# Transfer pieces at other places, the gated output's first product ahead of the stage boundary, tile differences and left remainders moved from GpSimd to VectorE

## The reference

```python
x = x + mixer(rmsnorm(x, norm_mix[i])) @ w_out[i]
h = rmsnorm(x, norm_ffn[i])
g = causal_dwconv(h @ w_gate, conv_w, conv_b)          # D_FF = 2816
x = x + (gelu(g) * (h @ w_up)) @ w_down
gate = sigmoid(rmsnorm(x, norm_ple[i]) @ w_ple_gate[i])
x = x + gate * (p[i] @ w_ple_proj[i])                  # p: 1024 x 256
```

## Time and profile before

| | |
|---|---|
| median of 3 runs | 3132.71 us (3130.48 to 3138.84) |
| the profiled execution | 3134.82 us, span of the core 3133.0 us |
| TensorE busy in the span | 3009.1 us (96%), weight loads 2506.6 us (80%) |
| VectorE, ScalarE, GpSimd busy | 2253.6 (72%), 1440.7 (46%), 1392.6 us (44%) |
| mean granted clock of TensorE | 0.988 of full speed |
| right-sum transfers, GpSimd's queue | 24 pieces, 1408 KB, median 10.2 us to landing |
| gate weights of the up pass | 11 loads a layer, 1024 KB, median 7.4 us to landing |

### The profile page before, as it was taken

How to read it: one execution, slowest core, us unless ns; L and a number is a source line. 1 busy time by engine, 2 the same in 40 slices (tenths; PEclk the granted TensorE clock), 3 DMA queues, 4 the chain that set the end, 5 groups by cost and what they waited for, 6 DMA issues and landing times. The chain is left out here.

```text
span 3133.0 us, 44207 instructions
## 1 busy us (share of the span) xinstructions
PE 3009.1 (96%) x14830; PEld 2506.6 (80%) x14830; DVE 2253.6 (72%) x3461; ACT 1440.7 (46%) x3127; POOL 1392.6 (44%) x913
## 2 busy tenths in 40 slices
PE   7999999999999989999999999999999999999999
PEld 6778888988877778878788887899877777877877
DVE  5599997888377778789943331999557677789962
ACT  4384537878243333344432211888443333344441
POOL 3105545564245555524322544676235555543330
PEclk9999999999999999999999999999999999999999
DMA  5313334222324552475311334323123564266511
GB/s 179 124 56 105 95 122 102 47 65 64 135 77 154 136 128 84 133 264 183 97 55 41 105 98 142 76 65 74 54 82 126 155 129 114 92 210 221 160 59 50
DMA packets 288086, 349.07 MB, mean 111 GB/s; under 512 B 88316, under 2 KB 181292, under 8 KB 287916
## 3 DMA queue, kind: packets, MB, share of 16 engines
q1 hardware_dynamic: 274860, 312.27, 31.7%
q0 software_dynamic: 13056, 34.60, 5.2%
HBM read 268.70 MB, written 112.20 MB: 122 GB/s over the span
## 5 line engine op out<-in xcount | busy, mean ns | idle before, releaser
L2171 DVE TENSOR_SCALAR_CACHE_REDUCE k_x<-k_x,l0in_cand,l0in_want 128x384 bf16<-128x384 f32 (+1 forms) x186 | 174.9, 1003 | 1.2 <-DVE l0in_before L2166 0.2
L2661 POOL TENSOR_TENSOR l0ff_w_lo<-l0ff_raw_g,l0ff_w_hi 128x512 fp32r<-128x512 f32 x64 | 90.3, 1414 | 163.2 <-ACT l0ff_w_hi L2519 162.1
L2661 POOL TENSOR_TENSOR l1ff_w_lo<-l1ff_raw_g,l1ff_w_hi 128x512 fp32r<-128x512 f32 x64 | 90.3, 1414 | 161.4 <-ACT l1ff_w_hi L2519 160.3
L78 PE MATMUL l1in_acc<-k_w_lo,k_hi 128*128 128x512 f32 x384 | 150.9, 393 | 2.4 <-PEq L99 2.4
L79 PE MATMUL l1in_acc<-k_w_hi,k_lo 128*128 128x512 f32 x384 | 150.1, 391 | 0.0
L80 PE MATMUL l1in_acc<-k_w_hi,k_hi 128*128 128x512 f32 x384 | 150.0, 391 | 0.0
L2548 ACT ACTIVATE k_x<-k_x 128x512 f32<-128x512 f32 x88 | 55.6, 631 | 170.9 <-DVE k_x L2753 170.9
L2709 DVE TENSOR_TENSOR l0ff_w_lo<-l0ff_raw_u,l0ff_w_hi 128x512 fp32r<-128x512 f32 x65 | 62.2, 957 | 83.0 <-ACT l0ff_w_hi L2519 83.0
L2709 DVE TENSOR_TENSOR l1ff_w_lo<-l1ff_raw_u,l1ff_w_hi 128x512 fp32r<-128x512 f32 x65 | 62.2, 957 | 79.7 <-ACT l1ff_w_hi L2519 79.7
L721 DVE TENSOR_TENSOR l1in_sq<-l1in_out 128x512 f32<-128x512 f32 x32 | 38.4, 1202 | 107.9 <-ACT l1in_out L658 107.5
L1632 DVE TENSOR_TENSOR l1dil_pt_lo<-l1dil_ring,l1dil_pt_hi 128x512 fp32r<-128x512 f32 x192 | 101.9, 553 | 4.7 <-ACT l1dil_pt_hi L1568 2.3
(11 more groups left out here) (663 smaller groups left out, 11291.6 us busy)
## 6 DMA issues: line engine op xcount, KB each, us to landing
l_right_sums<-in_w_down POOLq DMA_DIRECT2D x24, 1408.0 KB, 10.2
acts<-k_x SPq DMA_DIRECT2D x88, 256.0 KB, 2.0
k_raw<-in_w_in_odd SPq DMA_DIRECT2D x24, 512.0 KB, 3.9
l0ff_raw_g<-in_w_gate SPq DMA_DIRECT2D x11, 1024.0 KB, 7.4
l0ff_raw_u<-in_w_up SPq DMA_DIRECT2D x11, 1024.0 KB, 8.7
l0ff_a<-acts SPq DMA_DIRECT2D x44, 256.0 KB, 5.4
l0ff_d_one<-in_w_down SPq DMA_DIRECT2D x44, 256.0 KB, 3.0
l1ff_raw_g<-in_w_gate SPq DMA_DIRECT2D x11, 1024.0 KB, 7.4
```

The costliest lines, as they stand in the source:

```text
L78: pe.matmul(out, a_hi, b_lo, start=start, stop=False)
L2171: tick(dve.tensor_scalar(hits[:, cols], score[:, cols], cand[:, i:i + 1].bitcast(F32), want[:, i:i + 1], ALU.is_ge, ALU.add, accum_out=exc ...
L2661: pool.tensor_tensor(buf.ring_lo[q % R][:], operand(q), buf.ring_hi[q % R][:].bitcast(F32), ALU.subtract).then_inc(w_lo_done[0], 1)
```

## The change

1. The twelve right-sum pieces of a layer are issued at n = 2 and 12 of groups 1 to 6 (copies 1 to 3, adds 4 to 6).
2. The first gate product of `ple_stage` (24 matmuls) is done by TensorE at the end of `ffn_stage`, once tiles 0 and 1 and the gate weights' first half are ready. A pair of banks, `gate_bank`, lives across three stages for that: in the output stage it takes the transposes of odd tiles, in the feed-forward stage it is the second half of the up banks, in the last one it is `ps_g`. Unit 0 of `ple_stage` leaves its gate product out.
3. In the output stage GpSimd makes the differences of tile 4 alone. VectorE's first `sums_of` in the feed-forward stage covers tiles 5 and 6 in instructions of twice the width.
4. From down step 6 on VectorE makes every left remainder, GpSimd none.

```diff
@@ output_stage
-        tp = st.ps("tp", [P, 4, 512])
-        banks = [[tp[:, 2 * i + h, :] for h in range(2)] for i in range(2)]
+        tp = st.ps("tp", [P, 2, 512])
+        banks = [[z[:, h, :] for h in range(2)] for z in (tp, spare)]
...
-            for t in range(NT // 2, NT // 2 + 2):
-                nfeed.differences(pool, t)
+            nfeed.differences(pool, NT // 2)
@@ ple_stage
-        ps_g = st.ps("ps_g", [P, 2, 512])
+        ps_g = buf.bank
...
                 act.wait_ge(filled, i + 1)
                 if i == 0:
+                    act.wait_ge(begun, 1)
...
-                for k in range(KD):
+                for k in range(KD if i else 0):
@@ ffn_stage
-        LOWS.append([n + (z >= 6 and z % 2 == who if who else not (z >= 6 and z % 2)) for who, n in enumerate(LOWS[-1])])
+        LOWS.append([n + ((z >= 6) == bool(who)) for who, n in enumerate(LOWS[-1])])
...
-        bank = [buf.bank, st.ps("bank_u", [P, 4, 512])]
-        ups = bank[1]
+        bank_u = st.ps("bank_u", [P, 2, 512])
+        ups = [z[:, i, :] for z in (bank_u, nxt.bank) for i in range(2)]
+        bank = [[buf.bank[:, i, :] for i in range(4)], ups]
...
-                if n in (6, 13) and grp < 6:
-                    i = 2 * (grp % 3) + (n == 13)
-                    right_sums.copy(pool, i) if grp < 3 else right_sums.add(pool, i)
+                if n in (2, 12) and 1 <= grp <= 6:
+                    i = 2 * ((grp - 1) % 3) + (n == 12)
+                    right_sums.copy(pool, i) if grp <= 3 else right_sums.add(pool, i)
...
-            def sums_of(t):
-
-                at = slice((t - NT // 2) * P, (t - NT // 2 + 1) * P)
+            def sums_of(t, end):
+
+                at = slice((t - NT // 2) * P, (end - NT // 2) * P)
...
-            sums_of(LAST - 1)
+            sums_of(LAST - 2, LAST)
...
             for z in range(Z):
                 down(z)
+            pe.wait_ge(n_lo_ready, KD // 2)
+            pe.wait_ge(nfeed.rested, 4)
+            for k in range(KD):
+                mm = mm3(pe, nxt.bank[:, 0, :], nxt.hi[:, nxt.slot(0), k, :], nxt.lo[:, nxt.slot(0), k, :], nxt.x_hi[0][:, k, :], nxt.x_lo[0][:, k, :],
+                         k == 0, k == KD - 1)
+            mm.then_inc(begun, 1)
```

More of the change, by code:

```diff
@@ L845, with __init__ @@
     ROOTS = 4
-    def __init__(self, st, hi, lo, gain, w_gate, w_proj, p_in):
-        self.p_in = p_in
+    def __init__(self, st, bank, hi, lo, gain, w_gate, w_proj, p_in):
+        self.bank, self.p_in = bank, p_in
         self.gain, self.w_gate, self.w_proj, self.hi, self.lo = gain, w_gate, w_proj, hi, lo
@@ L2350, in ffn_stage @@
         a22 = cells("a22", (34, 38, 66, 70, 8, 10, 12, 14, 20, 22, 24))
-        bank = [buf.bank, st.ps("bank_u", [P, 4, 512])]
-        ups = bank[1]
+        bank_u = st.ps("bank_u", [P, 2, 512])
+        ups = [z[:, i, :] for z in (bank_u, nxt.bank) for i in range(2)]
+        bank = [[buf.bank[:, i, :] for i in range(4)], ups]
         NF = len(buf.FACTORS)
-        out = lambda grp, f, m: bank[m][:, (NF * grp + buf.FACTORS.index(f) + 2 * m) % 4, :]
-        feed = SplitFeed(st, x, hi, lo, xt, [None, [ups[:, 0, :], ups[:, 1, :]]], ident, buf.gain, buf.norm, buf.AHEAD, buf.ROOTS, "f_")
-        nfeed = Feed(st, x, nxt.hi, nxt.lo, [[ups[:, 2 * i + h, :] for h in range(2)] for i in range(2)], ident, nxt.gain, nxt.norm,
+        out = lambda grp, f, m: bank[m][(NF * grp + buf.FACTORS.index(f) + 2 * m) % 4]
+        feed = SplitFeed(st, x, hi, lo, xt, [None, ups[0:2]], ident, buf.gain, buf.norm, buf.AHEAD, buf.ROOTS, "f_")
+        nfeed = Feed(st, x, nxt.hi, nxt.lo, [ups[0:2], ups[2:4]], ident, nxt.gain, nxt.norm,
                      slot=nxt.slot, tag="n_")
@@ L2814, in add @@
                     dve.wait_ge(added, ADDED[r])
-                dve.tensor_tensor(cols, cols, bank[r % 2][:, n % 4, :], how).then_inc(added, 1)
+                dve.tensor_tensor(cols, cols, bank[r % 2][n % 4], how).then_inc(added, 1)
             def low_left(z):
@@ L2967, in _ @@
             pe.wait_ge(feed.rounded, 2)
[L2968 removed]
+            pe.transpose(ups[1][:, 0:4 * NFB], cw4, ident[0:4 * NFB, 0:4 * NFB]).then_inc(cw_t, 1)
             for q in range(4, Q):
@@ L3047, in trunk @@
                 recycle(nc)
-            with Stage(nc, L + "ff") as fs, Stage(nc, L + "pg") as gs:
-                ple = PleBuffers(gs, chain_hi, chain_lo, a["norm_ple"][layer], a["w_ple_gate"][layer], a["w_ple_proj"][layer], a["p"][layer, 0])
-                buf = FfnBuffers(fs, a["norm_ffn"][layer], a["w_gate"][layer], a["w_up"][layer], kept)
-                kept_stored = [nc.alloc_semaphore(f"{L}_kept_stored{b}") for b in range(2)]
-                filled = nc.alloc_semaphore(f"{L}_filled")
-                output_stage(nc, L + "out", merged, out_buf, ident, x, buf, kept_stored, filled, a["x"][0] if even else None)
-                recycle(nc)
-                Stage.used.extend(kept_stored + [filled])
-                ffn_stage(nc, L + "ff", x, buf, ple, right_sums[layer], a["conv_w"][layer], a["conv_b"][layer], ident, acts, kept_stored, filled)
@@ L3057, in trunk @@
-            recycle(nc)
-            if even:
-                ple_stage(nc, L + "pg", x, ple, ident, nxt=heads)
-                recycle(nc)
-            else:
-                ple_stage(nc, L + "pg", x, ple, ident, final=out[0])
+            with Stage(nc, L + "gate") as bs:
+                gate_bank = bs.ps("bank", [P, 2, 512])
+                with Stage(nc, L + "ff") as fs, Stage(nc, L + "pg") as gs:
+                    ple = PleBuffers(gs, gate_bank, chain_hi, chain_lo, a["norm_ple"][layer], a["w_ple_gate"][layer], a["w_ple_proj"][layer], a["p"][layer, 0])
+                    buf = FfnBuffers(fs, a["norm_ffn"][layer], a["w_gate"][layer], a["w_up"][layer], kept)
+                    kept_stored = [nc.alloc_semaphore(f"{L}_kept_stored{b}") for b in range(2)]
+                    filled = nc.alloc_semaphore(f"{L}_filled")
+                    begun = nc.alloc_semaphore(f"{L}_begun")
+                    output_stage(nc, L + "out", merged, out_buf, ident, x, buf, gate_bank, kept_stored, filled, a["x"][0] if even else None)
+                    recycle(nc)
+                    Stage.used.extend(kept_stored + [filled])
+                    ffn_stage(nc, L + "ff", x, buf, ple, right_sums[layer], a["conv_w"][layer], a["conv_b"][layer], ident, acts, kept_stored, filled, begun)
+                recycle(nc)
+                Stage.used.append(begun)
+                if even:
+                    ple_stage(nc, L + "pg", x, ple, ident, begun, nxt=heads)
+                    recycle(nc)
+                else:
+                    ple_stage(nc, L + "pg", x, ple, ident, begun, final=out[0])
```

15 lines of the change are left out of this document (7 added, 8 removed).

## The result

| | before | after |
|---|---|---|
| median | 3131.9 us | 3092.6 us (3090.6 to 3096.6) |
| the profiled execution, span | 3134.8, 3133.0 us | 3093.5, 3091.7 us |
| VectorE, GpSimd busy | 2253.6, 1392.6 us | 2238.8, 1269.5 us |
| mean granted clock | 0.988 | 0.993 |

The ratio is 0.9872, with a 95% interval of 0.9854 to 0.989: 1.3% faster, 40 us. The forecast was 3078.4 us, 14 us too low, inside its range; the nearest case of the prediction is rival (a), 3092.

The account below looks back on a forecast made before the run. TensorE works nearly all the time, so only its waits and slow clock can be won. 3134.8 - 50.7 + 8.2 - 3.6 - 8.2 = 3080.5 us, 3078.4 on the median's scale; range 3062 to 3102.

Parts of the forecast that it names:

- rival (a): Up pass: the add's tail still holds up its gate load, gaining 37 us for 50.7, so 3092 us; chance 0.15.
- Part 1: Up pass: moved right-sum pieces let gate loads land in time, gaining 50.7 of 52.6 us lost in both layers.
- within the 9.8: Up pass: a gate load landing up to 9.8 us after issue does no harm to the next group's first product.
- bound of 52.6: Up pass: the most the moved pieces could gain, all the time lost in both layers, 52.6 us.
- The other bound, 37: Up pass: the least gain, 37 us, if three loads per layer each meet their add for half its length.
- Part 2: Gated output: the early product moves the boundary later and unit 2 waits for VectorE's multiplication; +8.2 us in both layers.
- The half clock: Gated output: TensorE's 4.7 us stand ahead of unit 2 brings the half clock, 2.4 us more in layer 0.
- Part 3: Output stage's end: VectorE ends sooner, the next stage begins 1.5 us earlier; -1.8 us per layer, -3.6 in all.
- a tile's chain that sets the pace: Head of the feed-forward stage: scale, transpose, round and remainder set the pace, leaving a gain of 1.8 us per layer.
- Part 4: Down pass: VectorE making all left remainders at 2.65 us a step speeds steps and shrinks a TensorE wait; -8.2 us.
- Rival (d): Down pass: VectorE stands every step until ScalarE has rounded the left operand; +85 us, so 3172 us; chance 0.05.

Follow-up runs that it names:

- adds_at_0: The changed kernel with one add per group at n = 0 of groups 4 to 9, copies left as they are: 3073.9 us, ratio 0.9801.
- sigmoid_first: The changed kernel with ScalarE's roundings of weight chunks 2 to 4 put behind the sigmoids of units 0 to 2: 3087.1 us, ratio 0.9845.

## Why the prediction came out as it did

**Part 1**: forecast -50.7, measured -42.3 alone and -38.1 in the changed kernel (U). The direction and most of the size were right: the six gate loads that meet an add land after 6.6 to 8.4 us, where 7.7 to 8.3 was said (the slowest two of layer 0 in the changed kernel, 1072.5 to 1075.5 and 1114 to 1118, of each the gate load):

```profile
l0ff_raw_g<-in_w_gate SPq DMA_DIRECT2D x1, 1024.0 KB, 7.7
```
```profile
l0ff_raw_g<-in_w_gate SPq DMA_DIRECT2D x1, 1024.0 KB, 8.4
```

That this figure came out is in part luck. The undisturbed landing of 6.7 us was the slowest of eight loads in the kernel before with no piece in flight; the other seven took 5.3 to 5.6. The overlap with the add was 1.8 to 4.1 us, not 2 to 3, and it cost some 0.7 us per us in the changed kernel, not 0.5. The too high base and the too low price offset each other.

What failed is the step from "within the 9.8" to "gained". The slack was read for one consumer, product 0 of the next group, in a group that nothing had disturbed. Product 0 was on time; product 5, whose remainder VectorE makes, was not. I also asked only what the add does to the gate loads, and not to the stores, though the add of place 12 is in flight just when they go out. GpSimd's issue was priced at nothing, and with it at place 12 VectorE's next multiplication takes 3.9 to 4.4 us in place of 1.2. And I closed the account at group 7: the lag reaches the down pass, where the kernel before lost 2.6 and 1.1 us as well, so that U could shrink by 56.3 us (adds_at_0), more than my bound of 52.6. The other bound, 37 for loads that meet half an add, came close for a reason that isn't the one given.

**Part 2**: forecast +8.2 against a gain that the edit is meant to bring. Measured about +8.9 by the stretches. The chain was named rightly: it starts at the boundary, not at the product, and unit 2 starts 17.2 us behind the boundary in layer 0 (17.3 was said for the multiplication's end), after a wait of 2.75 us, and of 4.41 in layer 1, where 4.7 was said. The half clock was counted behind this wait in layer 0 too; in this execution it came there in layer 1 alone, where unit 2's product, 5.5 us at full clock, took 8.07 (window, busy us by engine, then the clock, the share of transfer engines and GB/s):

```profile
2984.00:2992.07 8.07, 8.07 (x25) 6.40 (x25) 5.96 (x6) 1.63 (x3) 2.37 (x1) 0.67 0.42 130
1559.93:1565.51 5.58, 5.58 (x24) 4.61 (x25) 5.54 (x6) 1.64 (x3) 2.40 (x1) 1.00 0.64 188
```

The next stage began 5.9 us after the early product did (5.76 was said), the wait at the boundary was 0.33 us where the earlier trace rows had 2.85, and sigmoid_first shows the cause of the other one: ScalarE's queue.

**Part 3**: forecast -3.6, measured -2.9. VectorE's last operations before the boundary are at 0.68 us, where 1.74 stood in the earlier trace rows:

```profile
884.43 0.68 DVE L808 TENSOR_TENSOR l0ff_xt<-l0ff_xt 128x512 f32<-128x512 f32 x1
885.03 0.68 DVE L804 TENSOR_TENSOR l0ff_lo<-l0ff_xt,l0ff_hi 128x512 fp32r<-128x512 f32 x1
885.63 0.68 DVE L998 TENSOR_TENSOR l0ff_lo<-l0ff_xt,l0ff_hi 128x512 fp32r<-128x512 f32 x1
```

The rest of the step, a tile's chain that sets the pace behind the boundary, held too.

**Part 4**: forecast -8.2, measured -8.5 by the ratio when undone, -8.3 by V and W. Rival (d), VectorE waiting for ScalarE in every step, did not happen: those stands are 0.1 us.

**The sum.** -38.1 + 8.9 - 2.9 - 8.4 = -40.5 us; the spans differ by 41.3. The forecast's -54.3 is 13 too much, and 12.6 of that are part 1. Rival (a) came out at the right time, 3092, with the right suspect but a part of the mechanism only: of the 13 us, the loads' delay at place 2 is one part, and the stores' delay and VectorE's long multiplication at place 12 are the others. How they share is open, since each place alone, done in six groups, loses as much as both in three (U in the table).

## What to carry to other kernels

When a transfer is moved, ask what else of every kind, loads and stores, goes out while it is in flight, and who stands in a queue behind each; and look at what the other engines' operations beside its issue take. Where an engine feeds TensorE at near its own full load, a small delay isn't absorbed by the next product's slack but carried: read the slack at several products and over several groups, down to the next stage. And work put ahead of a barrier only pays if what comes behind it can follow sooner; look in the other engines' queues for a wait that stands ahead of the first instruction that uses it.
